# The lift of the latent keys and values, moved into the recurrence as jobs on a PSUM bank of its own

## The reference

```python
c   = rms_norm(c_kv, kv_norm_g)          # (E, 128), E = 2064
k_h = w_uk[h] @ c ; v_h = c @ w_uv[h]     # 8 heads of 64
f = lb + (1 - lb) * sigmoid(f_raw); k = 1 - f
S_t = diag(f_t) S_{t-1} + k_t v_t^T ;  o_t = S_t^T q_t
y = concat([dsa_attention(...), rms_norm(o) * silu(gate_h)]) @ w_out
```

## Time and profile before

| | us |
|---|---|
| median of 3 runs | 3932.49 (3925.43 to 3934.19) |
| the profiled execution | 3917.86, span 3916.1 |
| recurrence, first load to the lift's first load | 2612.93 to 2897.70 |
| lift, first load to the attention's first load | 2897.70 to 3013.40 |
| TensorE, VectorE, ScalarE, POOL busy over the span | 3389.9, 2100.1, 1375.6, 896.2 |

### The profile page before, as it was taken

One profiled execution on the slowest core, in us unless ns is written; L12 is line 12 of the kernel. 1 busy time (PEld: TensorE's weight loads), 2 busy tenths in 40 slices (PEclk: granted clock), 3 DMA queues, 4 the chain that ended last, 5 costly groups with the idle time before them and its releaser, 6 DMA issues. The chain is left out here.

```text
span 3916.1 us, 44580 instructions
## 1 busy us (share of the span) xinstructions
PE 3389.9 (87%) x15839; PEld 2544.7 (65%) x15886; DVE 2100.1 (54%) x3972; ACT 1375.6 (35%) x2323; POOL 896.2 (23%) x819
## 2 busy tenths in 40 slices
PE   6898999699999996957999997957865998999798
PEld 4698888466666665845777775847742665666477
DVE  4200001466667774330889999947734554454466
ACT  3100001044444442220468874123451233333344
POOL 1120111155364441002322232323301112111100
PEclk9999999799999998978999998979977899999899
DMA  6221223665454424452212352441016545444454
GB/s 215 67 74 58 72 86 114 148 126 111 98 119 100 103 73 138 145 215 63 62 39 79 98 166 84 128 149 65 23 51 198 145 120 139 118 118 107 128 153 135
DMA packets 386852, 433.93 MB, mean 111 GB/s; under 512 B 113046, under 2 KB 302838, under 8 KB 374824
## 3 DMA queue, kind: packets, MB, share of 16 engines
q1 hardware_dynamic: 276044, 306.45, 28.0%
q10 hardware_dynamic: 104000, 86.95, 7.7%
q0 software_dynamic: 6592, 37.75, 3.4%
HBM read 298.41 MB, written 132.62 MB: 110 GB/s over the span
## 5 line engine op out<-in xcount | busy, mean ns | idle before, releaser
L2148 PE MATMUL f_pO<-f_PT,f_vv 128*128 128x512 f32 (+3 forms) x944 | 379.9, 485 | 21.4 <-ACT f_PT L2177 21.4
L2235 DVE CUSTOM_DVE_ANT_0 n_junk<-n_pM,n_chosen 128x512 bf16<-128x512 f32 (+4 forms) x352 | 200.7, 571 | 304.2 <-PE n_pM L2069 151.4
L2230 DVE TENSOR_REDUCE f_mxc<-f_pM 128x1 f32<-128x512 f32 (+2 forms) x448 | 240.0, 540 | 216.2 <-PE f_pM L2073 128.2
L2544 PE MATMUL cbank<-hT_high,cw_hi 128*128 128x512 f32 x800 | 322.6, 403 | 35.0 <-POOL kpartsI L2516 15.6
L2723 DVE TENSOR_SCALAR_CACHE_REDUCE sharedI<-xI,TI 128x384 bf16<-128x384 f32 (+8 forms) x284 | 348.9, 1294 | 0.1
L590 PE MATMUL p_bank<-hT_high,p_w_hi 128*128 128x512 f32 (+1 forms) x768 | 306.6, 399 | 44.4 <-POOL p_w_lo L556 39.4
L2177 ACT ACTIVATE f_PT<-f_pS 128x512 f32<-128x512 f32 (+3 forms) x472 | 220.9, 472 | 334.1 <-PE f_pS L2112 166.8
L2177 ACT ACTIVATE n_PT<-n_pS 128x512 f32<-128x512 f32 (+4 forms) x352 | 177.4, 504 | 426.1 <-PE n_pS L2127 365.2
L2148 PE MATMUL n_pO<-n_PT,n_vv 128*128 128x512 f32 (+4 forms) x704 | 313.6, 527 | 3.8 <-issue 1.1
L2544 PE MATMUL cbank<-hT_high,cw_lo 128*128 128x512 f32 x800 | 316.9, 396 | 0.0
L2544 PE MATMUL cbank<-hT_low,cw_hi 128*128 128x512 f32 x800 | 315.9, 395 | 0.0
(11 more groups left out here) (410 smaller groups left out, 7404.1 us busy)
## 6 DMA issues: line engine op xcount, KB each, us to landing
n_mkt<-scratch_mask_turned ACTq DMA_DIRECT2D x256, 128.0 KB, 2.1
cw_raw<-in_w_in_dram SPq DMA_DIRECT2D x50, 512.0 KB, 4.5
f_zz<-scratch_z SPq DMA_DIRECT2D x128, 128.0 KB, 3.0
p_w_raw<-in_w_in_dram SPq DMA_DIRECT2D x23, 512.0 KB, 4.0
wa<-in_w_ada_dram SPq DMA_DIRECT2D x8, 1024.0 KB, 5.4
xt<-in_x_dram SPq DMA_DIRECT2D x16, 512.0 KB, 6.8
scratch_z<-p_stage ACTq DMA_DIRECT2D x32, 256.0 KB, 2.4
scratch_qk_high<-p_stage ACTq DMA_DIRECT2D x32, 256.0 KB, 2.5
```

The costliest lines, as they stand in the source:

```text
L2148: pe.matmul(pO[:, B % 2, c0:c1], lhsT=vv[0:nk, b, kt, :], rhs=PT[0:nk, u % PR, c0:c1], start=(kt == 0 and not heads[h].local), stop=(heads ...
L2230: v.tensor_reduce(to, pM[:, n % 2, 0:wd], AX.X, ALU.max).then_inc(s_mx, 1)
L2235: v.tensor_tensor_reduce(junk[:, n % 2, 0:wd], pM[:, n % 2, 0:wd], chosen[:, at:at + wd], 1.0, 3.0 * NEG, ALU.add, ALU.max, accum_out=to). ...
L2544: last = pe.matmul(bank[:, p % RING, 0:wd], lhsT=w_part[pw][b][:, c, :], rhs=rhs, start=(c == 0 and a == 0), stop=(c == DC - 1 and a == 2))
```

## The change

`stage_lift` is gone. Its work becomes 79 jobs in the recurrence: 16 bias products, the turning of `w_uk`, 5 sums of squares, 20 high and 20 low key products, 17 value products. They are laid over 96 spots of `seq`, two in each step other than "prepare", "keys" and "queries", from level 1 of head 1 on: one behind the second group, one at the step's end. All use one new PSUM bank, `pL`; `pM` shrinks to one bank for it. For a job, TensorE waits until ScalarE has copied the job before it (`s_lx`), and ScalarE, at the same spot of its own program, waits for the product (`s_lp`) and copies it; SyncE's queue stores it at that step. A copy waits until the store two before it has landed.

Other parts: the low keys are no longer a subtraction on VectorE but a second product that adds minus the high part to what stands in the bank, copied by ScalarE. All pieces get their Ln first and one Exp (2064 columns), and VectorE one normalising product, behind level 6 of head 1. The bias columns are made two at a time. The values have one buffer `VT`; those of heads 1 and 3 are turned behind level 3, not ahead of level 1. ScalarE takes the sigmoids of heads 2 and 3 in its program's order, now behind jobs. The loads of heads 2 and 3 stand behind the jobs' stores of level 2. The state update waits for the meta keys of both heads of the pair.

Where the jobs fall: bias 0 to 15 from level 1 (head 1) to level 5 (head 0), with the values of head 1 among them; turning and squares in levels 5 and 6; high and low keys 0 to 19 from "turn" of head 1 to level 6 of head 3 (keys 16 to 19 have 16 columns); values 0 to 2 in level 7, 3 to 6 in "turn", 7 to 9 in "update", 10 to 13 in "out", 14 to 16 in "norm" of heads 2 and 3.

The diff, cut to its core; leading blanks are cut too:

```diff
-def stage_recur(nc, used, QH, FH, FHm, IV, IVm, lb_raw, norm_g, RR):
+def stage_recur(nc, used, QH, FH, FHm, IV, IVm, lb_raw, norm_g, RR, lift):
...
 b, last = a + 1, a + 2 == GH
 if a == 0:
     seq += [("prepare", a), ("keys", a), ("queries", a), ("prepare", b), ("keys", b), ("queries", b),
-            (0, a), (0, b), ("values", a), ("values", b)]
+            (0, a), (0, b), ("values", a)]
 for l in range(1, NL + 1):
     for h in (a, b):
         seq.append((l, h))
         if l == 1 and a:
             seq.append(("norm", h - 2))
+    if l == 3:
+        seq.append(("values", b))
     if l == 4 and not last:
         seq += [("prepare", a + 2), ("prepare", b + 2)]
 seq += [("turn", a), ("turn", b), ("update", a), ("update", b)]
...
     seq += [("out", a), ("out", b), ("norm", a), ("norm", b)]
 else:
     seq += [("keys", a + 2), ("keys", b + 2), ("out", a), ("queries", a + 2), (0, a + 2), ("out", b),
-            ("queries", b + 2), (0, b + 2), ("values", a + 2), ("values", b + 2)]
+            ("queries", b + 2), (0, b + 2), ("values", a + 2)]
...
+CK, CKm, kv_norm_g, w_uk, w_uv, rel_bias, bucket_tables, KTs, VE, BVs = lift
+PIECES = [(at, min(512, E - at)) for at in range(0, E, 512)]
+KEYS = [(j, at, wd) for at, wd in PIECES for j in range(4)]
+jobs = ([("bias", n) for n in range(2 * H)] + [("turn_uk", 0)] + [("squares", n) for n in range(len(PIECES))]
+        + [None] * 6 + [(part, n) for n in range(len(KEYS)) for part in ("high", "low")]
+        + [("values", t) for t in range(NE)])
+spots = [(step, h, spot) for step, h in seq if step not in ("prepare", "keys", "queries") for spot in range(2)][8:]
+assert len(jobs) <= len(spots)
+side = {}
+k = 0
+for n, job in enumerate(jobs):
+    if job is not None:
+        side[spots[n * len(spots) // len(jobs)]] = (k, *job)
+        k += 1
...
+square = bv[:, 0:2].rearrange("p z u -> p (z u)")[:, 0:512]
+lifted_high = m.sb("liftedhighL", [P, 2, 512], F32R)
+outs = m.sb("outsL", [P, E])
+scale, self_ = outs[:], outs[:, 0:5 * P].rearrange("p (l k) -> p l k", k=P)
+lifted_out, lifted_low = (outs[:, a:a + 1024].rearrange("p (z k) -> p z k", z=2) for a in (0, 1024))
+minus = m.sb("minusL", [P, P], F32R)
...
-F, KS, PW, VT = two("FG", [P, E]), two("KSG", [P, E]), two("PWG", [P, total]), two("VTG", [P, E])
+F, KS, PW, VT = two("FG", [P, E]), two("KSG", [P, E]), two("PWG", [P, total]), m.sb("VTG", [P, E])
...
 lraw, lexp, linv, lp, lb, oml = (m.sb(n, [P, GH]) for n in ("lraw", "lexp", "linv", "lp", "lbG", "omlG"))
 pG = m.ps("pGG", [P, 4, 4, P])
 pX = m.ps("pXG", [P, 2, 4, P])
-pM = m.ps("pMG", [P, 2, 512])
+pM = m.ps("pMG", [P, 512])
+pL = m.ps("pLG", [P, 512])
...
-if n:
-    sp.wait_ge(s_mv, rank("values", h - 2) + 1)
-sp.dma_start(VT[b][:, 0:S], IV[rows, :]).then_inc(s_vl[b], 16)
-sp.dma_start(VT[b][:, S:E], IVm[rows, :]).then_inc(s_vl[b], 16)
+if h:
+    sp.wait_ge(s_mv, rank("values", h - 1) + 1)
+sp.dma_start(VT[:, 0:S], IV[rows, :]).then_inc(s_vl, 16)
+sp.dma_start(VT[:, S:E], IVm[rows, :]).then_inc(s_vl, 16)
...
+def store_lifted(k, what, n):
+    sp.wait_ge(s_lx, k + 1)
+    if what == "bias":
+        sp.dma_start(BVs[n % 2][n // 2], bv[:, n % 2]).then_inc(s_bst[n % 2], 16)
+    elif what in ("high", "low"):
+        j, at, wd = KEYS[n]
+        z = what == "low"
+        src = lifted_low[:, n % 2, 0:wd] if z else lifted_high[:, n % 2, 0:wd].bitcast(F32)
+        sp.dma_start(KTs[z][j * P:(j + 1) * P, at:at + wd], src).then_inc(s_kst[n % 2], 16)
+    elif what == "values":
+        rows, at = latent(n)
+        sp.dma_start(VE[at, :], lifted_out[0:rows, n % 2, :]).then_inc(s_vst[n % 2], 16)
+n = 0
+for step, h in seq:
+    for job in lifted(step, h):
+        store_lifted(*job)
+    if (step, h) in ((2, 0), (2, 1)):
+        load(h + 2)
+    if step == "values" and h + 1 < GH:
+        load_values(h + 1)
+    if step == "norm":
+        for g in range(NG):
+            sp.wait_ge(s_res, NG * n + g + 1)
+            sp.dma_start(RR[h * GD:(h + 1) * GD, columns(g)], O[h % 2][:, columns(g)]).then_inc(s_st[h % 2], 16)
+        n += 1
+for b in range(2):
+    sp.wait_ge(s_kst[b], 32 * ((len(KEYS) + 1 - b) // 2))
+    sp.wait_ge(s_vst[b], 16 * ((NE + 1 - b) // 2))
+    sp.wait_ge(s_bst[b], 16 * H)
...
+own_.up(gp.tensor_scalar(minus[:], ident[:], -1.0, None, ALU.mult))
 own_.settle()
...
 act.activation(lexp[:], lp[:], ACT.Exp).then_inc(s_lb1, 1)
+def square_of(n):
+    at, wd = PIECES[n]
+    if n:
+        act.wait_ge(s_lp, job_no["squares", n - 1] + 1)
+    else:
+        act.wait_ge(s_in, 8 * 16)
+    act.activation(square[:, 0:wd], lat[:, at:at + wd], ACT.Square).then_inc(s_square, 1)
+def take_lifted(k, what, n):
+    act.wait_ge(s_lp, k + 1)
+    if what == "bias":
+        if n >= 2:
+            act.wait_ge(s_bst[n % 2], 16 * (n // 2))
+        act.activation(bv[:, n % 2], pL[:, 0:PITCH], ACT.Copy).then_inc(s_lx, 1)
+    elif what == "turn_uk":
+        act.activation(uk[:].rearrange("p j d -> p (j d)"), pL[:], ACT.Copy).then_inc(s_lx, 1)
+        act.wait_ge(s_const, 4)
+        for b in range(2):
+            act.wait_ge(s_bst[b], 16 * H)
+        square_of(0)
+    elif what == "squares":
+        at, wd = PIECES[n]
+        act.activation(scale[:, at:at + wd], pL[:, 0:wd], ACT.Ln, bias=eps[:, 0:1], scale=1.0 / RANK
+                       ).then_inc(s_lx, 1)
+        if n + 1 < len(PIECES):
+            square_of(n + 1)
+        else:
+            act.wait_ge(s_lx, k + 1)
+            act.activation(scale[:], scale[:], ACT.Exp, scale=-0.5).then_inc(s_root, 1)
+    elif what == "values":
+        rows = latent(n)[0]
+        if n >= 2:
+            act.wait_ge(s_vst[n % 2], 16 * (n // 2))
+        act.activation(lifted_out[0:rows, n % 2], pL[0:rows], ACT.Copy).then_inc(s_lx, 1)
+    else:
+        wd = KEYS[n][2]
+        if n >= 2:
+            act.wait_ge(s_kst[n % 2], 32 * (n // 2))
+        to = lifted_low[:, n % 2, 0:wd].bitcast(F32R) if what == "low" else lifted_high[:, n % 2, 0:wd]
+        act.activation(to, pL[:, 0:wd], ACT.Copy).then_inc(s_lx, 1)
+def beside(step, h, spot):
+    if (step, h, spot) in side:
+        take_lifted(*side[step, h, spot])
 def product_out(step, h, g, dst):
     k, n = group(step, h, g)
     act.wait_ge(s_px[k], n + 1)
...
+if g == 1:
+    beside(step, h, 0)
...
+beside(step, h, 0)
...
+        if g == 1:
+            beside(step, h, 0)
+elif step not in ("prepare", "keys", "queries"):
+    beside(step, h, 0)
+beside(step, h, 1)
...
+    if h >= 2:
+        v.wait_ge(s_lp, job_no["bias", 2 * h - 3] + 1)
+    v.tensor_scalar(rbB[:, h % 2, :], ones[0:BUCKETS], rb[:, h:h + 1], 8.0, ALU.mult, ALU.mult).then_inc(s_bv, 1)
+def normalise():
+    v.wait_ge(s_root, 1)
+    v.scalar_tensor_tensor(lat[:], lat[:], gl[:, 0:1], scale[:], ALU.mult, ALU.mult).then_inc(s_cn, 1)
...
-for step, h in seq:
+for at, (step, h) in enumerate(seq):
     b = h % 2
+    if at and seq[at - 1] in latent_at:
+        normalise()
+    for _, what, n in lifted(*seq[at - 1]) if at else ():
+        if what == "bias" and n % 2 and n // 2 + 2 < H:
+            bias_columns(n // 2 + 2)
...
+def beside(step, h, spot):
+    if (step, h, spot) not in side:
+        return
+    k, what, n = side[step, h, spot]
+    pe.wait_ge(s_lx, k)
+    if what == "bias":
+        pe.wait_ge(s_bv, n // 2 + 1)
+        last = pe.matmul(pL[:, 0:PITCH], lhsT=rbB[:, n // 2 % 2, :], rhs=tab[:, n % 2], start=True, stop=True)
+    elif what == "turn_uk":
+        for j in range(4):
+            last = pe.transpose(pL[:, j * P:(j + 1) * P], uk[:, j, :], ident[:])
+    elif what == "squares":
+        pe.wait_ge(s_square, n + 1)
+        wd = PIECES[n][1]
+        last = pe.matmul(pL[:, 0:wd], lhsT=ones[:], rhs=square[:, 0:wd], start=True, stop=True)
+    elif what == "high":
+        j, at, wd = KEYS[n]
+        pe.wait_ge(s_cn, 1)
+        last = pe.matmul(pL[:, 0:wd], lhsT=uk[:, j, :], rhs=lat[:, at:at + wd], start=True, stop=True)
+    elif what == "low":
+        wd = KEYS[n][2]
+        last = pe.matmul(pL[:, 0:wd], lhsT=minus[:], rhs=lifted_high[:, n % 2, 0:wd], start=False, stop=True,
+                         skip_group_check=True)
+    else:
+        rows, at = latent(n)
+        last = pe.matmul(pL[0:rows], lhsT=lat[:, at], rhs=uv[:].rearrange("p h d -> p (h d)"),
+                         start=True, stop=True)
+    last.then_inc(s_lp, 1)
...
 for c in range(4):
     last = make(k, 4 * g + c, c)
 last.then_inc(s_px[k], 1)
+if g == 1:
+    beside(step, h, 0)
...
 elif step == "values":
-    pe.wait_ge(s_vl[b], 32 * (h // 2) + 32)
...
+if h >= 2:
+    pe.wait_ge(s_m0, 2)
+pe.transpose(pM[0:NMETA, P:2 * P], VT[:, S:E], ident[:]).then_inc(s_mv, 1)
...
-pe.transpose(pM[0:NMETA, 0, 0:P], KS[b][:, S:E], ident[:]).then_inc(s_mk, 1)
+pe.wait_ge(s_mvc, 2 * (h // 2) + 2)
+pe.transpose(pM[0:NMETA, 0:P], KS[b][:, S:E], ident[:]).then_inc(s_mk, 1)
...
 elif step == "update":
-    pe.wait_ge(s_mkc, rank("turn", h) + 1)
-    pe.wait_ge(s_mvc, rank("values", h) + 1)
```

(37 more changed lines are left out.)

239 lines of the change are left out of this document (47 added, 192 removed).

## The result

The kernel after the change takes **3833.94 us** (median of 4 executions, 3832.39 to 3835.15) beside 3929.12 for the kernel before (4 executions, 3925.43 to 3934.19): ratio 0.9757, interval 0.974 to 0.9774, 95.2 us less on the medians. The profiled execution took 3833.1, its span is 3831.4. The prediction said 3849, in a range of 3830 to 3875: right in sign, 15 us too high.

The account below looks back on a forecast made before the run. The limit was seen as changing by stretch: VectorE in shallow levels, TensorE in deep levels and outputs, ScalarE's norm chain last. Removed stage -115.7 plus added work +32.6 gave -83.1 us, so 3849 from the median 3932.49; range 3830 to 3875.

Parts of the forecast that it names:

- fifth rival: Loads, barrier or last store of the removed stage still paid, or a lost head start: at most 5 us; chance 0.02.
- Start: Front of level 1: transposes of the second head's values leave it, -2.4 us; new loads and POOL's extra operation cost 0.
- Levels 1 to 4, heads 0 and 1: Shallow levels: TensorE replaces VectorE as limit, 4.95 us a step with two bias jobs; VectorE through near 2699, not 2695.9.
- Sigmoids in line: Level 5: sigmoids of heads 2 and 3 stand behind level 4's jobs on ScalarE, delaying level 5's copies: +2.2 us.
- Levels 6, 7, turn: Heads 0 and 1: +3.7 us for products on a full TensorE, +0.9 for the Exp ahead of level 7's copies.
- Outputs: Outputs with level 0 and values: key products less moved values, +3.0 us; last outputs: four values jobs, +3.6.
- Level 1 with norms: Most jobs hidden; one low copy and some 1.4 us of products ahead of the first norm: +2.0 us.
- first rival: Jobs in TensorE's idle gaps keep its clock at 2.4 GHz, returning 5 to 7 us: 3843 us; chance 0.12.
- Levels 5 to 7 and the turn: Heads 2 and 3, TensorE nearly full: seven tail products (1.4 us) and values 0 to 6 (6.3): +7.7 us.
- third rival: TensorE waits at the one shared bank for ScalarE's copies, 0.3 us more a job: +24, 3873 us; chance 0.21.
- fourth rival: Each of 73 stores must land before the next job: +165, 4097 us, slower than before; chance 0.02.
- The second (+15): Nearly all jobs hidden in idle engines, half way to the lower bound: +15, 3832 us; chance 0.08.

Follow-up runs that it names:

- e5: The kernel before, unchanged, run and profiled once more: 3929.07 us; recurrence and lift together 399.5 us.
- e1: The kernel after with no jobs: no products or copies, raw latent stored in their place; 3808.33 us, ratio to before 0.9695.
- e4: The kernel after with ScalarE's sigmoids of heads 2 and 3 placed earlier, behind level 3 and the values of head 1: 3832.71 us.
- e6: The kernel after with the jobs of the norm steps moved to the other spots: 3839.26 us, ratio to before 0.9778.
- e2: The kernel after with 62 bias, key and value products cut to 16 columns, copies and waits unchanged: 3816.85 us, ratio to before 0.9725.
- e9: The kernel before with unread products filling four TensorE gaps: 3928.11 us, ratio to before 1.0008.

## Why the prediction was right, and where it was off

**The 15.1 us.** 9.9 are the sum of the added work (32.6 forecast, 22.7 measured); 3.4 are the median of before, 3932.49 from three executions and 3929.12 in the result; 1.8 are left, less than the spread of either kernel. That the two stages carry the difference, and the profile's distance from the median does not, was the right step: e5 shows it.

**Removed stage, -115.7: right.** e1 shows that the stages without jobs take 284.5, the recurrence alone as before. The fifth rival (something of the stage stays) falls.

**Start, -2.4: -4.9.** From the first load to the first product of level 1 it was 39.28 and is 34.40. 2.4 are the transposes, as forecast; the rest is level 0 of head 1 at 3.81 us instead of 6.43, behind a gap like the others'. No job stands there, and nine of ten such profiles don't show it: this execution had it by luck.

**Levels 1 to 4, heads 0 and 1: right in size, +6.0 against +5.5.** The bound changed from VectorE to TensorE as said. Two errors cancel there. A bias job takes 0.81 us, not 0.65: half of its time in the lift was too low a price. So a step of two halves and two jobs takes 5.58 (2675.80 - 2670.22) and not 4.95. On the other side, the sum kept the 10.07 us that level 2 took at the low clock. In the kernel after, the granted clock of this stretch is 1.00 and the halves of level 2 take 2.02 to 2.05 us, as those of levels 3 and 4 do, so this term was 2.8 us too high.

**Sigmoids in line, +2.2: +1.3.** What was late next was a wait for ScalarE's copies (3.89 us), as named, but in level 5 of head 1. The step missed that VectorE's gating of heads 2 and 3 stands there as a limit of its own (e4).

**Levels 6, 7, turn, +4.6: +4.1. Updates, 0: +0.3 and +0.1.** The chain stayed at 6.10 us a head, and the jobs fitted under it.

**Outputs, +3.0 and +3.6: +2.3 and +3.4.** A high product takes 0.86; a low one was priced at 0.23 by the earlier trace rows and takes 0.32 (2762.07 to 2762.39). Both errors are small and opposite.

**Level 1 with norms, +2.0: -0.4.** This is the step that failed in kind. I counted what the jobs add and nothing that they give back, and left the clock to the first rival. The jobs in the gap held 2.4 GHz, and the second norm's products took 3.60 us instead of 5.96. e6 takes it away, e2 keeps it with small jobs, e9 makes it in the kernel before, where it is worth 2.4 us of the stretch. That the forecast is off by the same 2.4 is no proof that nothing else counts: VectorE's products with the norm took 4.7 us less (above), and TensorE waited 5.3 for the bank in this stretch (1.27, 1.07 and 2.96). What these two add up to in the stretch was not measured.

So the first rival's mechanism was true, at two of the three places that its 5 to 7 us came from: the norm, and level 2, whose 2.8 us the sum of the added work had charged. Against the kernel before, level 2 gives nothing back, since VectorE set the time there: from its copies ahead of level 2 to its gating of head 2 it took 32.2 us in the kernel before, and 32.2 in e9 with level 2 at 7.31. The third gap, ahead of level 6, moved into level 5. The rival's chance of 0.12 was too low. The Trainium skill (TensorE: Matmul & The Clock Gate, Part 1) has the slow clock as the default that activity releases; these rows agree: 5.96 and 3.60 us for the same eight records.

**Levels 5 to 7 and the turn, +7.7: +5.2.** Seven tail products were priced at 0.2 and take 0.14 and 0.11 (2838.68 to 2838.82, 2840.61 to 2840.72); and the values jobs in the turn filled waits for ScalarE's and POOL's work (0.25, 0.71 and 0.25 us in the profile of before) that the forecast charged twice, once as wait and once as job.

**The jobs as a whole.** Their products hold TensorE for about 52 us (16 x 0.81, 37 f32 ones of 512 columns at 0.86 to 0.90, 16 x 0.32 and the small ones), near the 50 forecast. By e2, 13.9 of 36 us reached the end of the stage; by e1, all costs together 23.0.

**The third rival, a handshake of 0.3 us a job, falls:** 8.6 us of waits for the bank, 0.11 a job, and 9.1 us in the stage for everything that is not product (e2 less e1). With the waits for the squares TensorE stood 10.2 us there, just over the 10 that the prediction had named as a sign of being wrong; it was no sign of this rival. **The fourth, the store round trip, falls too:** in the kernel after, ScalarE waited for a store once, 4.6 us, and TensorE 0.9 behind it. The second (+15) was nearer to the measured 22.7 than the forecast's 32.6, against its chance of 0.08.

**The rule against the change** would have made the sum 2.8 higher. The table load of 1.28 us at 2715.50 is followed by the Ln at 2716.80, 0.02 us later: this trace shows no drain, and the sum without it was already too high.
